# Token gathers of two experts split into four visits to TensorE, with the weight sums' helpers on in those experts too

## The reference, cut to what matters

```python
def moe_swiglu(h, w_router, we_gate, we_up, we_down):
    ...
    top_v, top_i = lax.top_k(logits, TOP_K)
    top_w = jax.nn.softmax(top_v, axis=-1)
    gates = jnp.sum(jax.nn.one_hot(top_i, N_EXPERTS, dtype=jnp.float32) * top_w[..., None], axis=1).astype(h.dtype)
    for e in range(N_EXPERTS):
        y = y + gates[:, e:e + 1] * swiglu(x, we_gate[e], we_up[e], we_down[e])
```

## Time and profile before

| | us |
|---|---|
| median of 3 runs | 1331.53 (1330.41 to 1332.1) |
| the profiled execution's own time | 1330.48 |
| its span, first to last instruction | 1328.7 |
| PE busy | 1297.7 (98%) |
| DVE busy | 593.2 (45%) |
| ACT busy | 357.5 (27%) |
| POOL busy | 131.3 (10%) |

### The profile page before, as it was taken

How to read it: one execution, slowest core, us unless ns; L and a number is a source line. 1 busy time by engine, 2 the same in 40 slices (tenths; PEclk the granted TensorE clock), 3 DMA queues, 4 the chain that set the end, 5 groups by cost and what they waited for, 6 DMA issues and landing times.

```text
span 1328.7 us, 28221 instructions
## 1 busy us (share of the span) xinstructions
PE 1297.7 (98%) x12158; PEld 840.7 (63%) x12158; DVE 593.2 (45%) x955; ACT 357.5 (27%) x586; POOL 131.3 (10%) x136
## 2 busy tenths in 40 slices
PE   6999999999999999999999999999999999999996
PEld 4758799998858533456666654545666654556542
DVE  5435755555544514803813732561380381373413
ACT  3334644443434400100700610010160060061001
POOL 0120000000030000000401310000140140131000
PEclk9999999999999999999999999999999999999999
DMA  9999986654693999999999999999999999999991
GB/s 349 361 339 328 359 297 192 192 197 146 259 311 129 421 383 422 384 397 402 421 419 417 420 420 417 420 375 395 408 421 418 419 421 418 417 421 419 417 396 43
DMA packets 113618, 471.41 MB, mean 355 GB/s; under 512 B 10123, under 2 KB 48821, under 8 KB 77654
## 3 DMA queue, kind: packets, MB, share of 16 engines
q1 hardware_dynamic: 111152, 463.80, 88.5%
q10 hardware_dynamic: 1766, 3.70, 0.7%
q0 software_dynamic: 576, 2.10, 0.4%
HBM read 465.43 MB, written 4.13 MB: 353 GB/s over the span
## 4 chain that ended last, share of the span: by engine, by line
PE 92%; DVE 4%; DMA 2%; issue 1%; ACT 1%; POOL 0%; SPq 0%; DVEq 0%; POOLq 0%; ACTq 0%
PE ps L2330 40%; PE ps L2376 18%; PE ps L1917 4%; PE ps L1918 4%; PE ps L1919 4%; PE ps L2345 3%; PE ps L1867 2%; PE ps L1965 2%; DMA token_rows<-y_rows,rti 1%; PE ps L2138 1%; PE ps L2139 1%; PE ps L2140 1%; PE ps L1930 1%; PE ps L1931 1%; PE ps L1932 1%; PE ps L2253 1%
## 5 line engine op out<-in xcount | busy, mean ns | idle before, releaser
L2330 PE MATMUL ps<-ering,xg 128*32 128x512 f32 (+1 forms) x6144 | 585.0, 539 | 1.9 <-DVE sq L1711 1.9
L2330 PEld LDWEIGHTS ps<-ering,xg 128*32 128x32 f32 x6144 | 317.3, 109 | 263.3 <-issue 158.7
L2376 PE MATMUL ps<-ering,eT 128*32 128x512 f32 x1176 | 243.4, 593 | 0.0
L2376 PE MATMUL ps<-wsum,eT 128*32 128x512 f32 x392 | 182.8, 594 | 0.0
L1711 DVE TENSOR_TENSOR sq<-sg,ps 128x512 f32<-128x512 f32 (+1 forms) x48 | 29.7, 619 | 329.3 <-PE ps L2330 245.7
L1121 ACT ACTIVATE sg<-ps 128x512 f32<-128x512 f32 (+1 forms) x48 | 26.1, 544 | 539.0 <-PE ps L2330 539.0
L812 POOL TENSOR_TENSOR sq<-ering 128x512 f32<-128x512 f32 x70 | 96.4, 1377 | 725.3 <-DMA ering<-in_moe_w_down 584.0
L1185 DVE TENSOR_TENSOR low<-ring,high 128x1024 fp32r<-128x1024 f32 (+1 forms) x104 | 122.6, 1202 | 71.5 <-ACT high L851 71.3
L2376 PEld LDWEIGHTS ps<-ering,eT 128*32 128x32 f32 x1176 | 94.4, 110 | 49.1 <-issue 31.7
L1917 PE MATMUL ps<-hx,high 128*128 128x256 f32 x432 | 119.8, 277 | 2.3 <-DVE hx L1239 2.3
L1919 PE MATMUL ps<-hx,low 128*128 128x256 f32 x432 | 119.5, 277 | 0.0
(11 more groups left out here) (295 smaller groups left out, 1622.5 us busy)
## 6 DMA issues: line engine op xcount, KB each, us to landing
ering<-in_moe_w_down SPq DMA_DIRECT2D x112, 1024.0 KB, 13.0
ering<-in_moe_w_gate SPq DMA_DIRECT2D x64, 1024.0 KB, 11.2
ering<-in_moe_w_up SPq DMA_DIRECT2D x64, 1024.0 KB, 13.2
ering<-in_moe_w_gate SPq DMA_DIRECT2D x64, 768.0 KB, 10.2
ering<-in_moe_w_up SPq DMA_DIRECT2D x64, 768.0 KB, 11.6
ring<-in_w_ada SPq DMA_DIRECT2D x40, 1024.0 KB, 7.7
ring<-in_ffn_w_gate SPq DMA_DIRECT2D x11, 1024.0 KB, 6.6
ring<-in_ffn_w_up SPq DMA_DIRECT2D x11, 1024.0 KB, 9.6
```

The costliest lines, as they stand in the source:

```text
L2330: last = mm(ps[32 * c:32 * c + 32, bank, 0:width].rearrange("p (n r) -> p n r", r=64), xg[:, kk, at, 32 * g:32 * g + 32], w[t][:, c, :, :] ...
L2376: last = mm(ps[32 * group:32 * group + 32, bank, :], h, w, start=(n, x) in DOWN_BEGINS, stop=(n, x) in DOWN_ENDS, skip_group_check=True)
```

## The change

The gathers of a group go in four turns of two pieces, after blocks 4, 6, 8 and 10, in PSUM banks 1 and 2. GpSimd makes `wdif` in experts 0 and 3 as well, and ACT copies the operands of the sums there as well, through three banks (0, 3 and 4). ACT issues the taking of a turn's pieces behind the last copy of the block that follows the gather. `COPIED` is gone.

```diff
+COPY_BANKS_GATHER, GROUP_BANKS = (0, 3, 4), (1, 2)
-COPIED = [e for e in range(NE - 1) if e not in GROUPS]
+GATHER_AFTER = (4, 6, 8, 10)
+GATHER_TURNS = len(GATHER_AFTER)
...
-            for k in COPIED:
+            for k in range(NE - 1):
                 pool.wait_ge(Y_row_ready, 1 + 2 * k)
...
+            def take_group(group, turn):
+
+                act.wait_ge(gat_done, gathers_before(group[0], 0) - GATHER_TURNS + turn + 1)
+                for m, bank in enumerate(GROUP_BANKS):
+                    A(xg[:, 2 * turn + m, group[0] % TOGETHER:group[-1] % TOGETHER + 1, :],
+                      ps[:, bank, 0:len(group) * CAP].rearrange("p (e t) -> p e t", t=CAP), ACT.Copy).then_inc((xg_first_ready, xg_last_ready)[m], 1)
...
                 for at in range(COPY_FIRST, W_SUMS * BLOCKS):
                     n, j = divmod(at, W_SUMS)
...
-                    if at >= COPY_FIRST + len(COPY_BANKS):
-                        act.wait_ge(wsum_ready, W_SUMS * BLOCKS * k + at - len(COPY_BANKS) + 1)
-                    bank = COPY_BANKS[at % len(COPY_BANKS)]
-                    if bank == UP_BANKS[0]:
-                        act.wait_ge(eh_ready, k * NSTEP * SG + SG + 2)
+                    if at >= COPY_FIRST + len(banks):
+                        act.wait_ge(wsum_ready, W_SUMS * BLOCKS * k + at - len(banks) + 1)
+                    bank = banks[at % len(banks)]
+                    if bank in UP_BANKS and at < COPY_FIRST + len(banks):
+                        act.wait_ge(eh_ready, k * NSTEP * SG + SG + G_ORDER[1].index(bank - UP_BANKS[0]) + 1)
                     b11, b12, b21, b22 = quarters(n)
                     A(ps[:, bank, :], (b12, b22, b21)[j], ACT.Copy).then_inc(wcopy_ready, 1)
+                    if k in GROUPS and j == W_SUMS - 1 and n - 1 in GATHER_AFTER:
+                        take_group(GROUPS[k], GATHER_AFTER.index(n - 1))
...
-                if k in COPIED and own >= COPY_FIRST:
-                    dve.wait_ge(wcopy_ready, COPIES * COPIED.index(k) + own - COPY_FIRST + 1)
-                    x = ps[:, COPY_BANKS[own % len(COPY_BANKS)], :]
+                if own >= COPY_FIRST:
+                    banks = copy_banks(k)
+                    dve.wait_ge(wcopy_ready, COPIES * k + own - COPY_FIRST + 1)
+                    x = ps[:, banks[own % len(banks)], :]
                 V.tensor_tensor(wsum[:, at % W_PLACES, :], x, y, ALU.subtract).then_inc(wsum_ready, 1)
-                if j == 0 and k not in COPIED:
-                    if n >= 2:
-                        dve.wait_ge(pieces_used, k * E_ITEMS + (MP0 + E_ITEM["d", 0, 0] + n - 1))
-                    V.tensor_tensor(wdif[:, (BLOCKS * k + n) % 2, :], b22, b12, ALU.subtract).then_inc(wdif_ready, 1)
...
+                            if rnd == 0 and e in GROUPS and (0, n0)[s] + i in GATHER_AFTER:
+                                gather_group(GROUPS[e], GATHER_AFTER.index((0, n0)[s] + i))
```

More of the change, by code:

```diff
@@ L111 @@
 GROUPS = {0: (1, 2, 3), 3: (4, 5, 6, 7)}
-COPIED = [e for e in range(NE - 1) if e not in GROUPS]
+GATHER_AFTER = (4, 6, 8, 10)
+GATHER_TURNS = len(GATHER_AFTER)
 def gathers_before(e, rnd):
     if rnd:
-        return 1 + 2 * len(GROUPS) + NE * (rnd - 1) + e + 1
-    return 1 + 2 * sum(e >= group[0] for group in GROUPS.values())
+        return 1 + GATHER_TURNS * len(GROUPS) + NE * (rnd - 1) + e + 1
+    return 1 + GATHER_TURNS * sum(e >= group[0] for group in GROUPS.values())
 COMBINE = ((0, 0, 6), (1, 0, 7), (0, 1, 6), (1, 1, 7))
@@ L506, in quarters, with copy_banks @@
             return w[:, 0, 0:512], w[:, 0, 512:1024], w[:, 1, 0:512], w[:, 1, 512:1024]
+        def copy_banks(k):
+            return COPY_BANKS_GATHER if k in GROUPS else COPY_BANKS
         def arrived_quarters(eng, k, n):
@@ L1124, in expert @@
                             take_xg(gathers_before(e + 1, rnd))
-                    elif e in GROUPS:
-                        take_group(GROUPS[e])
                     elif not ends:
@@ L2240, in gather_group @@
                 if turn:
-                    n = gathers_before(group[0], 0) - 1
+                    n = gathers_before(group[0], 0) - GATHER_TURNS + turn
                     pe.wait_ge(xg_first_ready, n)
@@ L2247, in gather_group @@
                     pe.wait_ge(h2l_ready, 2)
-                for m in range(4):
-                    out = ps[:, GATHER_BANK + m, 0:len(group) * CAP].rearrange("p (e t) -> p e t", t=CAP)
+                for m, bank in enumerate(GROUP_BANKS):
+                    out = ps[:, bank, 0:len(group) * CAP].rearrange("p (e t) -> p e t", t=CAP)
                     for b in range(2):
                         for part in (h2h, h2l):
-                            k = 4 * turn + m
+                            k = 2 * turn + m
                             last = mm(out, part[:, b, k * 128:(k + 1) * 128], P1[:, group[0]:group[-1] + 1, b, :],
@@ L2417, in expert @@
                                 pe.wait_ge(eh_ready, k * NSTEP * SG + NSTEP * SG)
[L2418 to L2425, removed]
+                            if rnd == 0 and e in GROUPS and (0, n0)[s] + i in GATHER_AFTER:
+                                gather_group(GROUPS[e], GATHER_AFTER.index((0, n0)[s] + i))
+                        if s == 0 and rnd and not ends:
+                            gather(e + 1, rnd)
                 expert(0, begins=True)
```

## The result

The changed kernel takes 1345.97 us (median of 4 runs, 1344.04 to 1346.32), the kernel before 1331.24 (4 runs beside them); the ratio is 1.011, 95% interval 1.0094 to 1.0125. That is 14.7 us slower, where 3.35 were forecast, and outside the range that I gave. Its profiled execution has a span of 1343.7 us, 15.0 above the span before.

A forecast was written before the change was run, and what follows sets the result against it. PE, busy 98% of the span, was taken as the bound. Rounds and visits +3.0, DVE's lighter load -0.45 and ACT's wait +0.8 gave +3.35 us on 1331.53, so 1334.9 us, range 1331.9 to 1338.5.

The forecast's parts named there:

- the paragraph on POOL's differences: Experts 0 and 3: 28 more GpSimd differences of 1.29 us each, hidden behind PE, cost nothing.
- the last cut leaves 0.75 rounds half filled: Expert's end: 33 matmuls over four column groups leave 0.75 rounds idle, part of 2.5 lost rounds an expert.
- the four cases: Slower by the sum (chance 0.57), no measurable change (0.23), much slower (0.12), faster (0.08).
- The rounds: Down product, four matmuls side by side, 0.858 us: one more round lost an expert, 0.86 us; 22-matmul stretches take 5.27 us.
- a visit: PE's switch to a gather and back: 0.32 us each beyond half-filled rounds; two more an expert, 0.64 us.
- DVE's lighter load: Experts 0 and 3: 14 differences leave DVE in each, so PE's losses to late sums go, -0.45 us.
- The tally: Down products of experts 3 and 0 against expert 1: 0.30 and 0.15 us left over as PE's loss to late sums.
- ACT's wait ahead of its copies: ACT waits at the taking with copies queued behind; m4 late in blocks 8 and 12, +0.8 us in all.
- rounds and visits: Experts 0 and 3: one more lost round and two more gather visits each, +3.0 us together.
- Much slower: Rival, chance 0.12: ACT's wait stalls sums beyond what half rounds hide, 5.6 instead of 0.8; +8.2 us, 1339.7.
- Faster: Rival, chance 0.08: PEld's waits for DVE are PE's full loss and half-filled rounds cost nothing; -4.1 us, 1327.4.
- no change: Rival, chance 0.23: DVE's lighter load also wins up to 0.9 us an expert, repaying 1.8 of 3.35; +1.6 us, 1333.1.

The follow-up runs named there:

- the kernel with three memsets: The changed kernel plus three small GpSimd memsets ahead of each weight difference from block 2 on: 1334.99 us, ratio 1.0026.
- The kernels with the change but without the loss: The changed kernel with GpSimd computing only 32 of 512 columns of each difference (1335.04 us), or with three GpSimd memsets ahead of each difference (1334.99 us).
- the stretches of 9.90 and 10.34 above: Expert 0's stretches of 44 matmuls in the kernel before with its first turn after block 3 instead of 4: 1331.02 us, ratio 0.9998.
- the first experiment: All of the change, but with the four turns after blocks 4, 5, 6 and 7: 1338.02 us, ratio 1.0049.

## Why the prediction was wrong, step by step

**The step that failed** is the paragraph on POOL's differences. It booked 28 more differences at nothing, read the 1.49 us of POOL beside 0.35 of DVE as a small loss that GpSimd alone has, and took it for a law of the two instructions. It was one side of a coin: the rows showed only the case in which DVE had started first, by 0.01 us, and I had both start times in front of me. Priced from rows, it would have been: DVE held for up to 1.29 us at a hidden sum, against 2.36 - 2.14 = 0.2 us of slack a block. The measured price is 2.05 us an expert in five experts, 10.3 us, and 0.6 in expert 3 (115.66 against 115.05 us, where GpSimd is late). This was missing from the sum whole; the place of the last cut set it off, as the kernel before with that cut alone shows (1341.53 us).

**Linked to it:** I worked out that the last cut leaves 0.75 rounds half filled and booked it as a cost, paid once. It also moves GpSimd's starts in the next experts, which my sum did not have at all, since the code there is the same. None of the four cases held this, so the range was cut at 1338.5.

**What held.** The rounds: stretches of 22 matmuls take 5.27 us, as forecast, and a visit with 8 gathers its share. The two experts with gathers: forecast +1.6 and +1.8 us, measured +1.3 and, where GpSimd is late (1334.99 us, the kernel with three memsets), 892.04 - 776.99 = 115.05 against 113.24, +1.8; with DVE held +2.4. The kernels with the change but without the loss are at 1335.04 and 1334.99, where the sum had 1334.9; against the kernel before beside them that is +3.9 and +3.45, where it had +3.35. That it comes so close is in part luck, as follows.

**Terms that were mis-sized and cancelled.** DVE's lighter load won more than 0.45. The first stretch of expert 0 went from 12.57 to 12.05 us. In expert 3, from the start of gate and up to the first gather, the kernel with three memsets takes 861.21 - 776.99 = 84.22 us against 858.45 - 773.87 = 84.58: 0.52 and 0.36, 0.88 together (in the changed kernel itself this part of expert 3 is 84.82, since DVE is held there). The tally had seen only what DVE's lateness cost beyond the half rounds, and the stretches of 9.90 and 10.34 above show that more lies hidden in them. ACT's wait ahead of its copies was forecast at 0.28 and 0.12 a block-8 or block-12 stretch, 0.8 in all; it measured 0.37 and 0.21 (5.64 and 5.48 against 5.27, and as much in the last stretches), 1.2 in all, and went away when the taking moved. That blocks 6 and 10 hide it was right. What is left for rounds and visits is 2.8 us, where 3.0 was forecast.

**The rivals.** "Much slower" was nearest in time (1339.7) and had a wrong mechanism: ACT's waits cost 1.2 us in all, not 5.6. "Faster" and "no change" counted on a lighter DVE, which is real but small.

## What to carry to other kernels

When instructions of DVE and GpSimd that both read SBUF overlap, read their start times in the trace, not only their durations, and in every repeat of the pattern, since the distance can drift: a pair that costs nothing now, with starts 0.01 us apart, may cost a full instruction after any change that moves either. Moving a cut in one expert changed the starts in the experts behind it; so look there too, where the code is the same. A wait hidden in idle rounds comes out when the rounds are filled, so such two gains are to be priced together, not one by one.

## What the runs showed of the hardware that was not expected

- A DVE instruction of 0.35 us with both inputs in SBUF took 1.16 to 1.48 us when it started 0.02 to 0.35 us after a GpSimd instruction of 1.28 us that reads SBUF, and ended 0.20 to 0.22 us after GpSimd's end. When it started first it took 0.35, and GpSimd's took 1.49 us if it came 0.01 us later, 1.35 at 0.14 and its usual 1.29 at 0.22 and beyond. Sums with one input in PSUM stayed at 0.68 beside the same instruction.
- A few hundredths of a microsecond can be 10 us: memsets of 0.06 us on DVE, 20 in all, which moved a start by 0.03 us, made the kernel 10.6 us slower by the medians, and three on GpSimd ahead of each difference made the changed kernel 11 us faster.
- Against DVE's first hidden sum, POOL's start came some 0.15 us earlier from expert to expert, with the same instructions in each; why stays open. A transpose of DVE that took 0.72 us instead of 0.58 in expert 5 of the first experiment was not what turned the order: DVE's sum started at 79.6 us as ever, and expert 3 of that run turned with its transposes at 0.58 and 0.59 (POOL, then DVE):

```profile
855.56 1.28 POOL L817 TENSOR_TENSOR sq<-ering 128x512 f32<-128x512 f32 x1 [0.75 <-PE ps L2376]
...
855.67 1.39 DVE L1600 TENSOR_TENSOR h_last<-eT 128x192 f32<-128x192 f32 x1
```
